# A recurrent mixer's matrix inverse on one core: both chains' small products issued in one burst, and what each chain owns of four PSUM banks

## The reference, cut to what matters

```
def step(state, inp):
    r_t, w_t, k_t, v_t, a_t, b_t = inp
    sa = jnp.einsum('bhvk,bhk->bhv', state, a_t)
    state = (state * w_t[:, :, None, :] + sa[..., None] * b_t[:, :, None, :]
             + v_t[..., None] * k_t[:, :, None, :])
    return state, jnp.einsum('bhvk,bhk->bhv', state, r_t)
```

## Time and profile before

| what | value |
|---|---|
| median of 3 runs | 2433.4 us (2431.77 to 2434.08) |
| the profiled execution's own time | 2433.51 us |
| its span, first to last instruction | 2431.7 us |
| PE busy | 2354.1 us, 97% |
| DVE busy | 1466.6 us, 60% |
| ACT busy | 1130.2 us, 46% |
| POOL busy | 196.6 us, 8% |
| mean granted TensorE clock | 0.995 |
| mixer, first layer | from 1500.76 us to 1683.85 us |
| mixer, second layer | from 2018.64 us |

### The profile page before, as it was taken

The page is one execution under the profiler, slowest core; times in us unless marked ns, Lnnn a source line. Parts: engine busy times, 40 slices in busy tenths (PEclk is TensorE's granted clock), DMA queues, the critical chain, the costliest instruction groups (busy, mean ns, idle before and its releaser), DMA issues.

```text
span 2431.7 us, 38846 instructions
## 1 busy us (share of the span) xinstructions
PE 2354.1 (97%) x16401; PEld 2027.3 (83%) x16401; DVE 1466.6 (60%) x1852; ACT 1130.2 (46%) x1566; POOL 196.6 (8%) x200
## 2 busy tenths in 40 slices
PE   7999999999999999999999999999999999999997
PEld 7777777888888888888888899889888898899885
DVE  4899966756554554454444456745655668456556
ACT  5565556644454444444333335423544545334542
POOL 4000000002000000000000001310000151301000
PEclk9999999999999999999999999999999999999998
DMA  9544455555565565666555575334547664335465
GB/s 242 155 158 148 155 192 153 161 191 182 187 190 185 189 190 187 190 187 190 190 190 191 186 226 173 114 98 122 157 129 242 171 217 139 97 106 150 136 203 170
DMA packets 260366, 415.77 MB, mean 171 GB/s; under 512 B 53448, under 2 KB 74440, under 8 KB 259424
## 3 DMA queue, kind: packets, MB, share of 16 engines
q1 hardware_dynamic: 254496, 395.63, 52.5%
q0 software_dynamic: 5376, 17.56, 2.4%
q10 hardware_dynamic: 320, 0.08, 0.0%
HBM read 406.90 MB, written 7.87 MB: 171 GB/s over the span
## 4 chain that ended last, share of the span: by engine, by line
PE 81%; DVE 12%; ACT 4%; issue 2%; DMA 1%; ACTq 0%; SPq 0%; DVEq 0%
PE banks L583 79%; DVE wp_hl L1159 4%; ACT wp_hl L1836 2%; DVE u_z L1490 1%; DVE nsd L1553 1%; ACT L1836 1%; DVE u_z L1472 0%; DVE r_SA L1694 0%; PE banks L695 0%; DMA raw<-w_in 0%; PE banks L707 0%; PE banks L820 0%; DMA xt<-x 0%; DVE xt L1471 0%; DVE r_SA L1660 0%
## 5 line engine op out<-in xcount | busy, mean ns | idle before, releaser
L1159 DVE TENSOR_TENSOR wp_hl<-raw,wp_hl 128x1024 fp32r<-128x1024 f32 x740 | 915.8, 1244 | 858.0 <-ACT wp_hl L1836 857.2
L1836 ACT ACTIVATE wp_hl<-raw 128x1024 fp32r<-128x1024 f32 x740 | 782.5, 1059 | 1081.6 <-PE banks L583 1058.7
L583 PE MATMUL banks<-wp_hl,XX_hl 128*128 128x512 f32 x3840 | 900.0, 393 | 10.2 <-DVE wp_hl L1159 10.2
L583 PEld LDWEIGHTS banks<-wp_hl,XX_hl 128*128 128x128 f32 x3840 | 715.8, 188 | 174.6 <-DVE wp_hl L1159 16.2
L583 PE MATMUL banks<-XX_hl,wp_hl 128*128 128x256 f32 x4992 | 646.3, 286 | 9.7 <-DVE wp_hl L1159 7.5
L583 PEld LDWEIGHTS banks<-XX_hl,wp_hl 128*128 128x128 f32 x4992 | 609.8, 191 | 30.7 <-issue 16.7
L583 PE MATMUL banks<-wp_hl,FF_hl 128*128 128x512 f32 x1056 | 240.7, 389 | 0.0
L583 PEld LDWEIGHTS banks<-wp_hl,FF_hl 128*128 128x128 f32 x1056 | 197.9, 188 | 41.0
L583 PE MATMUL banks<-wp_hl,MM_hl 128*128 128x512 f32 x384 | 88.4, 390 | 0.0
L583 PE MATMUL banks<-wp_hl,MXa_hl 128*128 128x512 f32 x384 | 88.3, 389 | 0.0
L583 PEld LDWEIGHTS banks<-wp_hl,MXa_hl 128*128 128x128 f32 x384 | 72.1, 188 | 15.0
(11 more groups left out here) (439 smaller groups left out, 1785.7 us busy)
## 6 DMA issues: line engine op xcount, KB each, us to landing
raw<-w_in SPq DMA_DIRECT2D x304, 512.0 KB, 3.8
raw<-w_out SPq DMA_DIRECT2D x96, 512.0 KB, 4.4
raw<-w_ffn_gate SPq DMA_DIRECT2D x88, 512.0 KB, 3.5
raw<-w_ffn_up SPq DMA_DIRECT2D x88, 512.0 KB, 3.5
raw<-w_ffn_down SPq DMA_DIRECT2D x88, 512.0 KB, 3.5
raw<-w_proj_attn SPq DMA_DIRECT2D x16, 512.0 KB, 4.4
raw<-w_proj_ssm SPq DMA_DIRECT2D x16, 512.0 KB, 4.4
raw<-w_glu SPq DMA_DIRECT2D x8, 512.0 KB, 3.7
```

What stands on the lines that cost most here:

```text
L583: return e.matmul(o, lhsT, rhs, start=start, stop=stop, skip_group_check=True)
L1159: return tt(d, src, hi, SUB)
L1836: return e.activation(o, x, func, bias=bias, scale=scale)
```

## The change

Both chains' stages of a turn are issued behind each other with no main steps between, and the main steps of both shares follow. This holds for all turns, on all engines. In turns 11 to 17 the odd ones run chain 1 first, so that the stage with `xx` and `xt` always precedes the other chain's `p`. The further main step between `xx` and `xt` is gone, and the even stages' share grows from 0.25 to 0.75. In the levels banks 4 and 5 now take `p` and `xx` of both chains and banks 6 and 7 take `xt` of both; chain 0 has columns 0 to 255 and chain 1 the others. PE no longer waits for its own `xx` ahead of `xt`. DVE's one addition becomes two: the one to `XT`, and the one to `X`, which also waits until ACT has copied the other chain's `p` out of the same banks. A bank can now have several marks (`beside`).

More of the change, by code:

```diff
@@ L491, in program @@
     RT = [marks(f"rw_t{c}", "l1", "l2", "kk", "kr", "rk", "vt", "pb0", "pb1", "ta", "tb", "pk0", "pk1", "tk", "L0", "q",
-                "p1", "xx1", "xt1", "p2", "xx2", "xt2", "p3", "xx3", "xt3", "p4", "xx4", "xt4", "p5", "xt5",
+                "p1", "xt1", "p2", "xt2", "p3", "xt3", "p4", "xt4", "p5", "xt5",
                 "au0", "au1", "rf0", "rf1", "s0", "s1", "s2", "y0", "y1", "mean", "var", "vr") for c in range(2)]
```

## The result

The changed kernel takes 2441.26 us (median of 6 runs, 2440.44 to 2442.05), beside 2432.55 for the kernel before (6 runs, 2430.45 to 2434.08). The ratio is 1.0035, 95% interval 1.0025 to 1.0045: 8.7 us slower, where 2.7 were forecast. That is inside the stated range of 2427 to 2443, but outside the 2430 to 2440 of the forecast's own mechanism; it is the time of the first rival. The profiled execution took 2440.9 us, 2439.1 of it the span, at a mean granted clock of 0.990 (0.995 before).

A forecast was written before the change was run, and what follows sets the result against it. TensorE, busy for 97% of the span, was taken to bound the kernel. The turns' terms summed to +0.45 us a layer, 0.9 for both; with 1.7 for one clock fall, 2433.5 became 2436 us, range 2427 to 2443.

The forecast's parts named there:

- the forecast's own mechanism: Whole kernel: the turns' terms plus one clock fall give 2436 us, own range 2430 to 2440, chance 0.47.
- the first rival: Turns 2 and 28, both layers: the clock falls at most long waits; four falls give 2441 us; chance 0.29.
- The sum without the clock: All turns of a mixer: gains and losses add up to +0.45 us a layer, 0.9 for both.
- Turns 1 to 3, forecast +5.7: Mixer start: joined stages lengthen VectorE's queue ahead of the weight splits, +5.7 us a layer, bounds 4.8 and 6.8.
- The wait of turn 2: Turn 2: PE's seventh step waits 4.3 us for a split queued behind both chains' stages, instead of 1.32.
- Turns 4 to 9, forecast -1.7: Behind turn 3: six boundaries between bursts and steps go, and the `r_PB` wait, -1.7 us a layer, bounds -0.4 and -2.4.
- Levels, forecast -5.0: Turns 10 to 18: joined bursts and vanished waits save 5.0 us a layer, bounds -3.8 to -5.3.
- Just inside one step: Levels: ACT's copy and DVE's addition to `X` take 1.5 us, covered by one main step of 1.63.
- Turns 19 to 28, forecast +1.45: Mixer end: seven boundaries save 1.7 us in turns 19 to 27; turn 28 costs 3.15, each layer.
- the position of step 63: Turn 26: job `ch` ends there; its convolution and chain 0's last stage delay chain 1's `rv`, a 3.7 us wait.
- I count one fall in all: +1.7: Whole kernel: the granted clock falls once behind the new long waits, costing 1.7 us of work.
- `au` of chain 0: First layer, end of the levels: a sign of the forecast, its start should come near 1618.5.

The follow-up runs named there:

- Experiment 6: Kernel before with its levels (turns 10 to 18) untouched and both chains' stages joined in all other turns: 2448.88 us, ratio 1.0070.
- the seventh experiment: Kernel before with only the levels' shares cut to 0.5 and 0, moving 4 main steps a layer out, nothing joined: 2454.64 us, ratio 1.0092.
- the third experiment: Changed kernel with idle matmuls filling PE's two long waits, four in turn 2 and three in turn 28: 2432.54 us, ratio 1.0001.
- the fifth version: Changed kernel joined only in turns 5 to 25, with levels' shares of 1 and 1 so no main step leaves them: 2422.66 us, ratio 0.9956.
- the first experiment: Changed kernel with joining kept only in the levels (turns 10 to 18), own shares in all other turns: 2444.15 us, ratio 1.0046.
- the second: Changed kernel with joining kept only in turns 4 to 25, own shares in the first and last turns: 2434.78 us, ratio 1.0006.
- the fourth: Changed kernel with own shares in turns 26 to 28, turns 0 to 25 still joined: 2445.05 us, ratio 1.0049.
- eighth: The fifth version plus four idle matmuls ahead of the longest wait between the two layers: 2421.51 us, ratio 0.9954.

## Why the prediction was right, and where its size was off

**The sum without the clock held, in part because errors cancel.** I had +0.45 a layer. Two mixers are 8.1 longer, 7.9 of that the clock's: about +0.1 a layer, and with the waits filled the whole kernel is at 2432.5. Turns 1 to 3 were put too high and the levels' gain too high as well, each by about 1 us. Step by step, relative to the first mixer's start:

*Turns 1 to 3, forecast +5.7:* turn 4 starts 43.5 us in, instead of 36.9: +6.6, of which 2.3 are the slow clock's. The wait of turn 2 was forecast at 4.3 and is 4.08, for the reason given: the timeline of DVE has chain 0's stage 2 (until 1521.48), then chain 1's stage 1, and the splits only then.

```profile
1521.48 1.22 DVE L1644 TENSOR_TENSOR_SCAN r_AQ<-cst,r_SA 128x512 f32<-128x512 f32 x1
...
1524.26 3.44 DVE L1167 TENSOR_TENSOR wp_hl<-raw,wp_hl 128x1024 fp32r<-128x1024 f32 x3
...
1534.41 0.81 DVE L1665 TENSOR_TENSOR r_AR<-rx,r_y 128x512 f32<-128x512 f32 x1 [0.98 <-ACT r_y L1843]
```

The wait of turn 3 is 1.50, not 2.8. Part of that is a slip: the terms of the prediction, from 1530.0 on, add up to 1541.2 and not to the 1541.7 that it goes on with. PE's own lateness doesn't shorten the wait (with the waits filled it is 1.5 too). ACT's lateness is 0.98, where I took 0.9; but from the bonus product to the split's end DVE needs some 10.3 us and not the 11.2 of my sum, the products at L1665 and L1668 taking 0.81 and 0.69 where chain 0's took 1.78 each, and the pair at L1673 1.91 instead of 0.87. In the rows of POOL every one of the long ones has a product of POOL beside it (from 1515.02, 1516.98, 1518.48, 1535.17 and 1536.96); that it is the cause was not tested.

*Turns 4 to 9, forecast -1.7:* -1.6 (6.6 down to 5.0 at turn 10). Experiment 6, where the same turns are joined, has the gain in them as well. The page of the Trainium skill that I weighed (TensorEngine Tiling (Array Packing), Key Properties: a change of mode drains TensorE) would have left 0.66 of it for the two pairs of 64x64 tiles. The wait of 0.4 for `r_PB` is gone as well; the 1.1 that remain of the measured 1.6 speak for some gain at the mixed boundaries too, about 0.5 for all four, though not by an experiment of its own.

*Levels, forecast -5.0:* -4.1. A burst takes 2.01 (2.02 forecast). The timeline of PE in the first level:

```profile
1577.64 0.69 PE L589 MATMUL banks<-r_kb,r_SA 64*64 64x64 f32 x32
...
1579.65 1.70 PE L589 MATMUL banks<-XX_hl,wp_hl 128*128 128x256 f32 x12
1581.59 0.69 PE L589 MATMUL banks<-r_kb,r_SA 64*64 64x64 f32 x32 [0.24 <-issue]
```

What is missing is behind the four single steps: from step to burst they take 1.94, 2.03, 1.83 and 2.03, not 1.63, 1.3 in all where I had allowed 0.4. Two of the four (at 1590.70 and 1608.74) wait 0.33 for the addition to `X`. "Just inside one step" was too tight for the copy and the additions.

*Turns 19 to 28, forecast +1.45:* +2.3, of which 1.6 are the slow clock's, so +0.8 without it; in the second layer, which had no wait for issue to lose, +3.3 and +1.8. The wait on `r_rv` is 3.63, where I had 3.7. My reason was the position of step 63, and the seventh experiment shows just that: moved alone, it makes a wait of 4.8; left in place (experiments 5 and 6) it is 1.7.

*The step that failed: "I count one fall in all: +1.7".* There are four in the mixers, that is the first rival: the wait of 3.6 is enough as well, and both recur in the second layer. Four falls cost 7.9 in their groups and the fifth, between the layers, became longer; the third experiment gives 8.7 for the four. The rival's 2441 is the time measured, in part by luck: it has 6.8 for four falls, where 7.9 to 8.7 were measured, and the 1.5 between the layers and the 2.1 ahead of the mixers are in no sum. I had let the shortness of 3.7 beside 4.35 speak against it, and the prediction says that the trace has one long wait between busy stretches. It has two. The other, of 3.72 us, stands at 75.62 in the first block of the kernel before, and the granted clock falls behind it, to 5.1 us short of full clock in all:

```profile
75.62 0.45 PE L757 MATMUL banks<-cst,BP 128*128 128x128 f32 x1 [3.72 <-issue]
```

```profile
74.00:78.00 4.00, 1.31 (x6) 0.97 (x8) 3.77 (x8) 1.26 (x5) 0.00 (x0) 0.51 0.29 100
```

The same trace has waits of 1.67 and 1.71 (1704.57 and 1791.29) with no fall behind them. So the trace at hand had the price of a wait as long as the one forecast in turn 28. By the Trainium skill (TensorE: Matmul & The Clock Gate, HAM oscillation) recurring idle gaps pay the fall each time; by that rule the forecast would have been 2441, and the trace of the changed kernel agrees.

*A hit by luck.* `au` of chain 0 was forecast near 1618.5 and starts at 1618.43. Counted from the mixer's start it comes 119.8 us in, where 117.7 were forecast: 2.0 late, mostly the slow clock's 2.3 of turn 2, and hidden by the start of the mixer, 2.1 earlier.

**What gives the gain back.** The joined bursts do bring what was counted, and the change spends it twice: on DVE's queue in turns 1 to 3, and on the four main steps that it moves out of the levels, which were cover there and bring `ch` against `rv` at the end. Joining only turns 5 to 25 and keeping the steps gives 10 us, nearly all of it in the levels.

**Open.** Whether the new levels alone, with full shares and every other turn as before, give all of the 10 us, which no run tried; whether joining the last turns would help the fifth version too; and why some falls are twice as long as others behind the same wait (next section but one).

## What to carry to other kernels

- A wait of PE has two prices: its length, and the slow clock behind it. Before a change trades several short waits for one long one, price the fall too, from rows at either clock; single waits under 2 us cost only themselves here. Look for such rows in the whole trace, also far from the place of the change.
- Work that is issued in one piece pays where the other engines have it ready. Join bursts where the engine behind them has slack, and leave them apart where its queue is the limit (here turns 1 to 3). The last turns are no such place in the changed kernel: left apart, they made it 4 us slower.
- Filler work that is moved out of a stretch must be followed to where it lands: its last step starts another job's tail, and what is queued behind that tail on VectorE waits.

## What the runs showed of the hardware that was not expected

- The granted clock fell behind every wait of PE of 3.6, 3.7, 4.1, 4.35 and 4.8 us between stretches of matmuls, unless it was filled (only at the very start, with one matmul ahead, do the rows show 1.00 behind a wait of 5.4), and behind no single wait of up to 1.7; but it fell behind 1.73 and 1.49 with one group of 1.09 between them (the sixth experiment, both layers). In between it varied: of four waits of 2.10 in the seventh experiment one was followed by a fall, and in the first experiment the one of 2.13 was and the one of 2.30 was not.
- A fall shows as about 1.7, 3.4 or 5.1 us short of full clock (windows of 1 us, one less the granted clock, summed). The same wait of 4.35 us between the layers had 1.7 before, 3.4 after and in the first, sixth and seventh experiments, and 5.1 in the second to the fifth; the same wait of 3.7 at 75 us had 5.1 before and in the fourth and eighth, and 3.4 in the others. Nothing in the rows tells why.
- Four idle matmuls of 512 columns (3.6 us) in a wait of 4.1 kept the clock at 1.00, though 0.64 of waiting were left; three with 1.06 left did as well.
